# Attention jobs on one core: VectorE's softmax front of the next job is put ahead of the reciprocal of the job before

## What is computed

```
s_band = einsum(q, k_window) * scale + bias     # learned bias, -inf outside the window
s_ctx  = einsum(q, k_ctx) * scale
p = softmax(concat([s_band, s_ctx]))
o = p_band @ v_window + p_ctx @ v_ctx
```

## Time and profile before

| | |
|---|---|
| median of 3 runs | 2965.26 us (2964.52 to 2968.98) |
| profiled execution | 2968.76 us, its span 2967.0 us, mean granted TensorE clock 0.988 |
| busy share of the span | PE 96%, DVE 60%, ACT 37%, POOL 9% |
| stretch of the jobs behind the global ones | 743.89 to 820.19 us |

### The profile page before, as it was taken

The page is one execution under the profiler, slowest core; times in us unless marked ns, Lnnn a source line. Parts: engine busy times, 40 slices in busy tenths (PEclk is TensorE's granted clock), DMA queues, the critical chain, the costliest instruction groups (busy, mean ns, idle before and its releaser), DMA issues. The chain is left out here.

```text
span 2967.0 us, 47144 instructions
## 1 busy us (share of the span) xinstructions
PE 2862.3 (96%) x19366; PEld 2707.3 (91%) x19366; DVE 1767.8 (60%) x2644; ACT 1107.4 (37%) x1750; POOL 254.9 (9%) x197
## 2 busy tenths in 40 slices
PE   8999999998799999999999999999989999999997
PEld 5999999986589999999999999999945698999997
DVE  6567666647666655667564646467778747332334
ACT  5311126446865211146211126653324436211123
POOL 0000002000020000010000001000038511000002
PEclk9999999999999999999999999999999999999999
DMA  6545443520044444443544434522211133322233
GB/s 227 163 152 182 143 152 132 158 67 28 23 128 142 156 133 139 150 151 120 163 147 131 142 114 133 175 91 79 84 48 33 55 103 121 114 83 67 72 106 114
DMA packets 106968, 350.33 MB, mean 118 GB/s; under 512 B 11137, under 2 KB 29825, under 8 KB 106497
## 3 DMA queue, kind: packets, MB, share of 16 engines
q1 hardware_dynamic: 101122, 338.27, 35.6%
q10 hardware_dynamic: 5632, 9.05, 0.9%
HBM read 336.66 MB, written 10.62 MB: 117 GB/s over the span
## 5 line engine op out<-in xcount | busy, mean ns | idle before, releaser
L1664 PE MATMUL P<-xh,wh 128*128 128x320 f32 x4016 | 1019.3, 313 | 8.9 <-DVE xl L1152 7.4
L1664 PE MATMUL P<-xl,wh 128*128 128x320 f32 x4016 | 1005.8, 310 | 0.0
L1664 PE MATMUL P<-xh,wl 128*128 128x320 f32 x4016 | 1005.1, 310 | 0.0
L759 ACT CAST wh<-raw 128x1024 fp32r<-128x1024 f32 (+1 forms) x431 | 482.1, 1119 | 965.2 <-PE P L1664 810.3
L1112 DVE TENSOR_TENSOR wl<-raw,wh 128x1024 fp32r<-128x1024 f32 (+1 forms) x431 | 564.8, 1310 | 294.0 <-ACT wh L759 293.4
L1664 PEld LDWEIGHTS P<-xh,wh 128*128 128x128 f32 x4016 | 696.2, 188 | 17.8 <-issue 7.6
L1664 PEld LDWEIGHTS P<-xl,wh 128*128 128x128 f32 x4016 | 696.4, 188 | 2.6 <-issue 0.2
L1664 PEld LDWEIGHTS P<-xh,wl 128*128 128x128 f32 x4016 | 696.1, 188 | 0.0
L1664 PE MATMUL P<-hh,wh 128*128 128x320 f32 x1408 | 382.4, 312 | 0.0
L1664 PE MATMUL P<-hl,wh 128*128 128x320 f32 x1408 | 377.0, 308 | 0.0
L1664 PE MATMUL P<-hh,wl 128*128 128x320 f32 x1408 | 376.8, 308 | 0.0
(11 more groups left out here) (240 smaller groups left out, 2446.5 us busy)
## 6 DMA issues: line engine op xcount, KB each, us to landing
raw<-wgu_d SPq DMA_DIRECT2D x216, 512.0 KB, 3.7
mraw<-wmod_d SPq DMA_DIRECT2D x128, 512.0 KB, 3.6
raw<-wdB_d SPq DMA_DIRECT2D x64, 704.0 KB, 4.2
raw<-wdA_d SPq DMA_DIRECT2D x32, 704.0 KB, 5.4
raw<-ain_d SPq DMA_DIRECT2D x28, 512.0 KB, 3.5
raw<-sz_d SPq DMA_DIRECT2D x26, 512.0 KB, 3.9
raw<-sx_d SPq DMA_DIRECT2D x24, 512.0 KB, 3.5
raw<-aout_d SPq DMA_DIRECT2D x16, 512.0 KB, 3.6
```

Of the source, the lines that this page charges most:

```text
L759: nc.scalar.copy(wh[:, u.u % SPLITS, 0:n], raw[:, u.u % 2, 0:n]).then_inc(hi_done, 1)
L1664: ins = nc.tensor.matmul(P[:, u.banks[i], 0:C], w[:, u.u % SPLITS, k * 128:(k + 1) * 128], m[:, k, C * h:C * h + C], start=(k == 0 and w i ...
```

## The change

VectorE's loop, and nothing else. In turns 17 to 39, whose job before is not a global one, `front(i)` is issued ahead of `shares(i - 1)`; in the other turns the order stays. The steps themselves, their waits, and the other engines' orders are the same.

```diff
             def attention(p):
                 for i in range(len(jobs) + 2):
+                    ahead = 1 <= i < len(jobs) and jobs[i - 1].kind != "gl"
+                    if ahead:
+                        front(jobs[i])
                     if 1 <= i <= len(jobs):
                         shares(jobs[i - 1])
-                    if i < len(jobs):
+                    if i < len(jobs) and not ahead:
                         front(jobs[i])
                     if i >= 2:
                         take(jobs[i - 2])
```

## The result

The changed kernel is slower: a median of 2973.82 us over 18 runs (2966.69 to 2978.58) against 2966.35 us (2962.59 to 2969.78), ratio 1.0025, interval 1.0019 to 1.0032. That is +7.5 us, outside my range of 2962.5 to 2971.0. The profiled execution took 2978.56 us. It is the second slowest of the 18, 4.7 us above their median, so what its profile shows is probably more than the median execution loses.

What follows compares the result with a forecast made beforehand. The prediction took the stage to be set by a ring of waits through ScalarE, with no engine full. It summed 0 removed and +0.9 us added to 2965.3, giving 2966.2 us, range 2962.5 to 2971.0.

Steps and rivals of the forecast that it cites:

- The prize: ScalarE's waits at the exponential for VectorE's negative maximum: 8.6 us in 16 pieces, the most the change could save.
- a take pins the new order: On VectorE, each moved front queues behind a take that must wait for TensorE's weigh; 3.31 us per job against 3.33.
- The wait that moves from exponential to scaling: ScalarE's wait shifts from the negative maximum to the reciprocal, worth the same in steady state; some 11 us over 23 turns.
- The walk by spacings: Turn-by-turn sum of profiled spacings in the stage: +1.05 us by job 21, +0.04 a head, last take about 0.9 later.
- T = S + 3.07: VectorE's take of a job starts 3.07 us after the next job's first exponential, behind TensorE's scores and weigh.
- rival (b): TensorE's clock falls to its lower level in sixteen nl jobs, costing 10.6 us, to 2975.9; chance 0.04.
- the new ring: Cycle of waits after the change: ScalarE, VectorE and also TensorE's scores and weigh, spanning two jobs; 6.63 us.
- 0.66 a job: Extra us per nl job at TensorE's low clock: a period of 3.99 us in a slow stretch, against 3.33.
- the old ring: Cycle of waits before the change, once around ScalarE and VectorE per job; 3.33 us for an nl job.
- nine turns: Number of further low-clock turns from which the slower clock would decide the result: 5.9 us / 0.66.
- 0.9 by my spacings: Forecast loss for the whole change: nothing removed, last take of the stage about 0.9 us later.
- rival (d): Forecast's mechanism, stronger: reciprocal late by 0.2 to 0.3 us more in 23 turns, +2.5 to +5.9, up to 2971; chance 0.08.

Runs made afterwards that it cites:

- late_take: Changed kernel with take moved one turn later as well; 2959.33 us against 2967.80 for the kernel before, ratio 0.9971.
- late_old: Kernel before, old order kept, with take alone moved one turn later; 2964.69 us against 2966.48, ratio 0.9995.
- not_last: Changed kernel with the front ahead in turns 17 to 35 only, the last head in the old order; 2970.05 us against 2966.48, ratio 1.0011.
- after_look2: Changed kernel run once more, unaltered, for a second profile; 2975.60 us in one run.
- gc_only: Kernel before with the front ahead in turns 17 to 20 alone; 2968.18 us against 2967.80, ratio 1.0003.
- fill_short: Changed kernel plus one spare matmul ahead of TensorE's transposes, 256 columns for nl jobs from turn 22, else 128; 2968.96 us against 2966.80, ratio 1.0009.
- fill_light: Changed kernel plus one spare matmul ahead of TensorE's transposes, 128 columns to turn 21, then 384 between nl jobs, else 256; 2972.82 us against 2966.48, ratio 1.0022.
- fill_light_look2: Kernel of fill_light run once more, unaltered, for a second profile; 2969.17 us in one run.

## Why the prediction was wrong, point by point

- The prize, and that a take pins the new order: right, shown by late_take (-8.5, where its expectation had -8) and late_old.
- The wait that moves from exponential to scaling: right in kind and size, 11.6 us.
- The walk by spacings, at full clock: right. At job 21 I had +1.05, and not_last has +1.07 (12.94 against 11.87); for a head I had +0.04, and after_look2 has -0.01. That gc_only needs 0.85 more to the first tile, worked out 0.6, is in part luck, since its profile and that of before each hold a low stretch of their own.
- The step that failed is the time of a take, T = S + 3.07, the one that the prediction trusted least. It was read from rows at full clock and used in every turn, and the sum had no term for TensorE's clock. At full clock it holds (S + 3.04); in a low turn it was S + 4.36. The prediction had asked only what an earlier take would bring.
- The lower clock was left to rival (b): its mechanism, "the new ring passes through scores and weigh, and gives TensorE gaps at other points", was named, and both its chance (0.04) and its price were wrong. I set against it that "TensorE's busy share stays the same, and one stretch out of a whole stage fell". The share does stay about the same; where the idle time lies doesn't. The new order leaves up to 1.36 us ahead of the transposes of an nl job, and near the nc job three gaps of 0.6 to 0.8 us in a row, and in the first profile the clock fell behind these once a head, at 777, 794 and 811 us. The rows of the first (idle time in brackets):

```profile
773.68 0.41 PE L1742 MATMUL P<-cst,pb 128*128 128x128 f32 x2 [0.77 <-ACT pb L882]
...
774.71 0.70 PE L1726 MATMUL P<-pt 64*128 64x256 f32 x4 [0.62 <-ACT pb L873]
...
776.75 1.29 PE L1742 MATMUL P<-cst,pb 128*128 128x128 f32 x6 [0.74 <-ACT pb L882]
...
784.65 0.84 PE L1742 MATMUL P<-cst,pb 128*128 128x128 f32 x6 [1.36 <-ACT pb L882]
```

  after_look2 has the same three gaps in the head from job 25 on (0.77, 0.62, 0.75 us), and there the clock stayed at 1.00. So these gaps alone don't settle it.
- The price per turn, "0.66 a job", came from the old ring, where the low clock touches little of the ring (turns of 3.33 in gc_only, of 3.34 and 3.99 in before). In the new ring scores and weigh both lie on it. With 1.3 us a turn (4.82 against 3.50) the point from which (b) decides is not nine turns but four or five (5.9 / 1.3), and fewer with the projection's start, which I left out: 1.3 us in the profiled execution.
- So the loss at the median is 0.9 by my spacings, and the other 6.6 are what is left over, not a measurement. That the clock is the cause of most of the 7.5 is shown by fill_short (same order, clock held, 5.3 us back) by the heads of after_look2 against those of the first profile, and by jobs 16 to 25, which take 28.2 and 28.3 us in the two profiles of the changed kernel, both with a low stretch there, and 25.2 in fill_short at full clock; the executions' clocks fit it. What is not shown is which gap makes it fall; the stretches lie differently in the two profiles.
- The price of rival (d) doesn't follow from its terms: 0.2 to 0.3 us in each of 23 turns is 4.6 to 6.9 us, where I wrote +2.5 to +5.9. In the turn shown above there is no such delay: the reciprocal came when I had it, at T + 2.33.
- Open: fill_light's median. Its two profiles show 3.1 and 1.8 us up to the first tile, its median 6.3 (interval 3.9 to 9.2). The rest of the execution, from the last take to the end of the span, is 2143.3 us in late_old's profile, 2146.8 in before's and 2150.7 in after's, with the same code, so a single profile can't settle it. Nor is it known whether the change costs something there: behind the first tile the two profiles of the changed kernel have 2146.3 and 2146.6 us against 2143.7, but late_take, the fastest of all, has 2146.3 too.

## What to carry to other kernels

Moving a step ahead of a wait puts what stood behind that wait behind the step, and the step behind whatever ended the last turn. Write down the new ring before the old one is cut, and move what pins it in the same change: front ahead and take later together gave -8.5 us, each alone +7.5 and about 0. And when a new ring takes in TensorE's work, price that ring at both of its clock levels, along with the dense work that follows.

## What the runs showed of the hardware

The same kernel ran one head in 15.8 us in one profiled execution (after_look2) and in 17.1 in another (after), according to the clock granted to TensorE; an exponential on ScalarE took 0.56 us in both. I had not expected it to fall at all here: TensorE's longest idle time in the stage was 1.4 us (1.6 for its weight loads), shorter than the 1.89 us ahead of the one low stretch of before, and it still was granted the lower level of 1.2 GHz in five stretches. With one short spare matmul per turn it was granted 2.4 GHz throughout the stage in two profiles of three (fill_short, fill_light_look2); in the third, fill_light's first, it fell once, at 757 to 761 us.
